# A hybrid decoder layer: another order for two mixers' products and copies, a down product with moving weights for one-tile experts, and a first projection tile by tile

## The chip, the cores and the metric

The kernel runs on one core of one Trainium2 chip. The metric is device time in microseconds (us). Engines are named as in the profile: PE is TensorE, DVE is VectorE, ACT is ScalarE, POOL is GpSimd, SP issues DMAs. All data are float32.

## What is computed

One layer for 1024 tokens of width 1024. The first part normalises the input and projects it; the columns of the projection feed two token mixers. The second part is a top-4-of-32 expert network.

```python
y = rmsnorm(h, norm_mix_g[l])
proj = y @ w_in[l]
u, v_gm, qkv, z, a, bb = jnp.split(proj, split_points, axis=-1)
out_a = gmlp_chunk_mixer(u, v_gm, gm_norm_g[l], gm_ws[l], gm_bs[l])
out_b = gated_deltanet_mixer(qkv, z, a, bb, conv_w, a_log, dt_bias, norm_g)
h = h + concatenate([out_a, out_b]) @ w_out[l]
h = h + moe_ffn(rmsnorm(h, norm_ffn_g[l]), router_w, router_b, w_gu, b_gu, w_down, b_down)
return rmsnorm(h, final_norm_g)
```

The gated DeltaNet runs over chunks of 128 tokens here. Per chunk and head it needs key-key and query-key products, the inverse of a unit lower triangular matrix (built in 7 levels, each doubling the block size), and then a step that reads the old state S, gives new values, and updates S. Each expert computes `((up + 1) * (gate * sigmoid(1.702 * gate))) @ w_down[e] + b_down[e]` for the tokens routed to it.

## The kernel before, in words

Each engine has its own instruction queue, written out by hand; semaphores tie the queues together. There are three blocks with a barrier between them.

**First block, projections.** SP loads constants, seven small parameter tensors, the eight tiles of x (128 tokens each), and then the weights of the v, u and z columns. ACT squares four tiles at a time (L312), DVE takes the mean and scales (L208, L466), POOL takes the root (L211), PE transposes (L393), and DVE copies out of PSUM into `yT` with the gain (L472). Only when all eight tiles are in `yT` does the projection begin: POOL copies each tile of `yT` into `ytile` (L270), and PE multiplies it with 512-column pieces of the weights (L408), eight products for each of v, u and z and eight narrow ones for the a and b columns. The chunk mixer's gate product (L414) closes each tile. Then come the q, k, v columns (L430) with their convolution.

**Second block, mixers.** Work goes in four pairs of chunks, i = 0 to 3, and a pair has slots s = 0 and 1 with four PSUM banks each. `start(i)` transposes the decays and betas into banks (L773, L776); `chunk(i)` makes Gk (L805) and Gq (L808), the transposed keys and values (L817, L821), the transposed lower matrix (L830), the levels (L763 and L837), and the state step: values and old state (L872, L873), state product, output (L882, L883), transposes of both mixers' outputs (L890, L894). `project` multiplies with w_out (L900). DVE turns Gk into LT (L973), Gq into AT (L975), scales keys and values (L980, L981, L983), begins the inverse (L989, L991) and updates the state (L1016). The router work of pair i-1 (`h_columns`, `logits`, `ranks`, `best_four`, `rows_of`) is spread over pair i.

**Third block, experts.** Experts are sorted by their number of tokens, and each of the 32 ranks has a fixed width: ranks 0 to 14 have two token tiles (224 down to 132 columns), ranks 15 to 31 one tile of 128. Per expert PE transposes the gathered rows (L1319), makes gate and up (L1340), and the down product (L1357). In the down product a 128 x 128 piece of the weights is stationary and the tokens' 128 columns move, so the result has features on partitions; ACT adds the bias (L1282), PE transposes back (L1328, eight of them per tile, inside the next expert's gate and up), DVE scales by the router's weight (L1477), and POOL scatters with an add (L1216). SP loads weights into six slots: each slot is loaded anew as soon as the expert before has used it (L1166 for gate and up, L1174 for down).

## Time and profile before

| quantity | value |
|---|---|
| median of 3 runs | 2508.07 us (2507.85 to 2508.09) |
| the profiled execution | 2509.08 us, of which the profile's span is 2507.2 us |
| PE busy | 2356.5 us, 94% |
| first block until the first projection product | 0 to 39.55 us |
| second block | 417.92 to 812 us |
| first transposes of the third block | 843.75 us |
| one-tile experts | about 1708 to 2472 us, 44.80 us each |

A product of float32 operands appears in the trace as two MATMUL records, a transpose as one. A row "x128" of L1357 is thus 64 products. In a timeline the distance between the starts of two rows is the time that the first took, because the end of the last instruction of a row overlaps the next. "Idle before" stands in square brackets with what ended it. PEclk is the granted TensorE clock: 1.00 is 2.4 GHz, 0.50 is 1.2 GHz.

### The profile page before, as it was taken

What the parts mean: (1) busy time and instruction counts of PE and PEld (TensorE: products, weight loads), DVE (VectorE), ACT (ScalarE), POOL (GpSimd) and SP (SyncE); (2) the same over time, 40 slices, a digit from 0 to 9 for tenths busy, and PEclk for the clock granted to TensorE, in tenths of its full rate; (3) what the DMA queues carried; (4) which work ended last, traced back from release to release, by engine and by line L of the source; (5) the groups of instructions that cost most, each with busy time, mean ns of one, the idle gap of its engine ahead of it and who ended that gap; (6) DMA issues with size and microseconds to landing.
All of it is one profiled execution on the core that took longest, in us unless ns stands there. A gap on an engine that the chain in (4) does not pass through costs nothing. (4 is left out here: it accounts for less than half of the span.)

```text
span 2507.2 us, 40183 instructions
## 1 busy us (share of the span) xinstructions
PE 2356.5 (94%) x16253; PEld 2090.4 (83%) x16254; DVE 703.4 (28%) x1627; ACT 400.7 (16%) x898; POOL 609.0 (24%) x808
## 2 busy tenths in 40 slices
PE   6999997998997599999999999999999999999994
PEld 3554444786784599999999999999999999999994
DVE  3112334445443215222222221222221212212122
ACT  2221552211211000101101111111111111111112
POOL 1112111124233312222222222232222222222222
PEclk8999999999999799999999999999999999999997
DMA  7000113010110676777788888989999999999974
GB/s 250 0 0 0 34 34 123 1 51 18 35 51 26 233 253 209 222 227 242 236 260 258 256 279 285 294 279 309 304 303 308 299 312 304 302 308 302 311 250 152
DMA packets 368902, 496.42 MB, mean 198 GB/s; under 512 B 11952, under 2 KB 281716, under 8 KB 368680
## 3 DMA queue, kind: packets, MB, share of 16 engines
q1 hardware_dynamic: 353976, 450.11, 53.9%
q0 software_dynamic: 14752, 43.84, 6.7%
q8 instruction: 127, 2.08, 0.4%
q14 instruction: 47, 0.39, 0.0%
HBM read 462.21 MB, written 34.13 MB: 198 GB/s over the span
## 5 line engine op out<-in xcount | busy, mean ns | idle before, releaser
L1340 PE MATMUL ps<-arena 128*128 128x128 f32 (+15 forms) x8192 | 1038.4, 288 | 0.8 <-DVE arena L1469 0.8
L1340 PEld LDWEIGHTS ps<-arena 128*128 128x128 f32 x8192 | 1029.6, 191 | 1.2 <-DVE arena L1469 1.0
L1357 PE MATMUL ps<-arena 128*128 128x128 f32 (+15 forms) x4096 | 521.3, 289 | 1.4 <-POOL arena L1228 1.4
L1357 PEld LDWEIGHTS ps<-arena 128*128 128x128 f32 x4096 | 515.7, 191 | 3.4 <-POOL arena L1228 1.8
L1493 DVE TENSOR_SCALAR arena<-ps,arena 128x128 f32<-128x128 f32 (+15 forms) x256 | 94.9, 371 | 1163.8 <-PE ps L1340 1160.6
L1225 POOL TENSOR_TENSOR arena<-arena 128x128 f32<-128x128 f32 (+15 forms) x256 | 133.0, 520 | 911.6 <-DVEq L1500 911.6
L1273 ACT ACTIVATE arena<-arena 128x128 f32<-128x128 f32 (+15 forms) x256 | 83.5, 326 | 1008.9 <-DVE arena L1493 1008.9
L408 PE MATMUL ps<-arena 128*128 128x512 f32 (+1 forms) x512 | 182.7, 513 | 3.9 <-POOL arena L270 3.5
L408 PEld LDWEIGHTS ps<-arena 128*128 128x128 f32 x512 | 89.0, 193 | 98.2 <-issue 94.4
L1282 ACT ACTIVATE arena<-ps,arena 128x128 f32<-128x128 f32 (+15 forms) x256 | 98.1, 383 | 448.9 <-PE ps L1357 448.9
L430 PE MATMUL ps<-arena 128*128 128x512 f32 x384 | 166.5, 592 | 0.0
L430 PEld LDWEIGHTS ps<-arena 128*128 128x128 f32 x384 | 72.8, 190 | 90.9 <-issue 90.9
L763 PE MATMUL ps<-arena 128*128 128x128 f32 x896 | 126.5, 299 | 20.4 <-DVE arena L991 14.2
L763 PEld LDWEIGHTS ps<-arena 128*128 128x128 f32 x896 | 119.8, 210 | 23.1 <-DVE arena L991 15.2
L1228 POOL TENSOR_TENSOR arena<-arena 128x128 f32<-128x128 f32 (+15 forms) x256 | 127.0, 496 | 20.1
L211 POOL TENSOR_TENSOR small<-small,cst 128x4 f32<-128x4 f32 (+1 forms) x34 | 31.0, 916 | 349.5 <-DVE small L208 349.4
L900 PE MATMUL ps<-arena 128*128 128x512 f32 x256 | 111.7, 593 | 0.0
L900 PEld LDWEIGHTS ps<-arena 128*128 128x128 f32 x256 | 47.9, 190 | 56.9 <-issue 56.9
L1494 DVE TENSOR_SCALAR arena<-ps,arena 128x128 f32<-128x128 f32 (+15 forms) x256 | 92.6, 362 | 0.0
L1203 POOL DMA_INDIRECT arena<-h_dram,arena x47 | 46.9, 998 | 176.4 <-DMA arena<-list_dram 166.0
L1216 POOL DMA_INDIRECT h_dram<-arena x47 | 74.6, 1586 | 31.9 <-issue 31.9
L1319 PE MATMUL ps<-cst,arena 128*128 128x128 f32 x376 | 48.1, 279 | 31.4 <-DMA arena<-h_dram,arena 31.3
(229 smaller groups left out, 1480.5 us busy)
## 6 DMA issues: line engine op xcount, KB each, us to landing
arena<-in_exp_w_gu SPq DMA_DIRECT2D x256, 1024.0 KB, 7.9
arena<-in_exp_w_down SPq DMA_DIRECT2D x64, 2048.0 KB, 9.1
arena<-in_x SPq DMA_DIRECT2D x16, 512.0 KB, 5.5
h_dram<-arena SPq DMA_DIRECT2D x16, 512.0 KB, 2.7
arena<-in_w_in SPq DMA_DIRECT2D x6, 1024.0 KB, 5.4
arena<-in_w_in SPq DMA_DIRECT2D x2, 2048.0 KB, 13.6
arena<-in_w_out SPq DMA_DIRECT2D x1, 4096.0 KB, 13.0
arena<-h_dram SPq DMA_DIRECT2D x8, 512.0 KB, 7.1
```

The source lines that it names most:

```text
L408: last = t_.matmul(bank(bk)[:, 0:width], ytile[s][:, k, :], wuvz[:, k, c0:c0 + width], start=(k == 0), stop=(k == KT - 1))
L430: last = t_.matmul(bank(2 * s + hf), wq[w][:, k, s * P:(s + 1) * P], yT[:, k, 512 * hf:512 * (hf + 1)], start=(k == 0), stop=(k == KT - 1))
L763: last = t_.matmul(out_bank[:, c], left[:, c], right[:, c], start=start, stop=stop)
L900: last = t_.matmul(bank(4 * s + 1 + n), mixT[s][:, k, :], wout[:, k, 512 * n:512 * (n + 1)], start=(k == 0), stop=(k == KT - 1))
L1225: v.tensor_tensor(gmn[m % 2][:, 0:n], gmn[m % 2][:, 0:n], umn[m % 2][:, 0:n], ALU.mult).then_inc(S("gum", m % 2), 1)
L1228: v.tensor_tensor(hT[:, m, 0:n], gmn[m % 2][:, 0:n], sg[m % 2][:, 0:n], ALU.mult).then_inc(S("hT"), 1)
L1273: a.activation(sg[m % 2][:, 0:n], gmn[m % 2][:, 0:n], ACT.Sigmoid, scale=ALPHA).then_inc(S("sg", m % 2), 1)
L1282: a.activation(yv[:, d, 0:n], bank(6 + d % 2)[:, 0:n], ACT.Identity, bias=bias[:, 16 + d:17 + d]).then_inc(S("yv"), 1)
L1340: last = t_.matmul(bank(m % 4)[:, q * CAP:q * CAP + n], wslot[g][:, k, 256 * q + c:256 * q + c + P], xT[:, k, 0:n], start=(k == 0), stop=( ...
L1357: last = t_.matmul(bank(6 + d % 2)[:, 0:n], wslot[g][:, k, c:c + P], hT[:, k, 0:n], start=(k == 0), stop=(k == KT - 1))
L1493: v.tensor_scalar(gmn[r][:, 0:n], bank(m % 4)[:, 0:n], of[:, m:m + 1], LIMIT, ALU.add, ALU.min).then_inc(S("gmn", r), 1)
L1494: v.tensor_scalar(umn[r][:, 0:n], bank(m % 4)[:, CAP:CAP + n], of[:, 8 + m:9 + m], LIMIT, ALU.add, ALU.min)
```

## The change

**First projection, tile by tile.** Tile 0 of x is loaded ahead of the parameters, tiles 1 and 2 between the weight loads, the rest behind them. Each tile is squared, scaled and transposed by itself; the transposes of tile t+1 stand on PE behind the v product of tile t. Products read `yT` directly, and POOL's copy into `ytile` is gone. Loops are unrolled.

**Mixers.** On PE: both Gk first, then Gq and the transposed lower matrix in turns, then the transposed values and keys. Scaled keys and values are made by ACT, per head, out of PSUM; only `ke` stays on DVE, moved to level 1. In the state step the value products of both slots come first, and the product of the queries with the old state stands between the new values' product and its use. DVE's state update no longer waits for the output product. Behind the chunk, PE runs: gates' transposes of slot 0, `start(i + 1, 1)`, values' transposes of slot 0, `start(i + 1, 0)`, the first half of slot 0's projection, both transposes of slot 1, its second half, ranks, slot 1's projection. DVE does slot 1's two copies behind `start(i + 1)`. At the end of the last pair, slot 1's residual stands ahead of `best_four(i, 0)` on DVE.

**One-tile experts.** The down product has the tokens stationary and 512 columns of the weights moving (two banks of eight products), so tokens are on partitions at once. ACT's bias step and PE's transposes back are gone. DVE adds a row of biases and then scales. SP loads that row for each of these experts, spread to 128 partitions (512 KB). Ranks 0 to 14 and the loop for overflowing experts stay as they were.

```diff
+            def load_x(t):
+                sp.dma_start(xr[:, t, :], x[0, t * P:(t + 1) * P, :]).then_inc(S("x_in", t), 16)
...
+            load_x(0)
...
+            load_x(1)
...
+            load_x(2)
...
+            for t in range(3, TT):
+                load_x(t)
...
-                    v.tensor_copy(ytile[s], yT[:, :, ds((2 * i + s) * P, P)]).then_inc(S("ytile", s), 1)
...
+            for t in range(TT):
+                if t + 1 < TT:
+                    x_root(t + 1)
+                pool.wait_ge(S("v_var"), t + 1)
...
+            def x_square(t):
+                act.wait_ge(S("x_in", t), 16)
+                if t >= 2:
+                    act.wait_ge(S("xT"), 2 * t - 2)
+                a.activation(xn[t % 2], xr[:, t, :], ACT.Square, accum_out=small[:, 20 + t % 4:21 + t % 4]).then_inc(S("x_ss"), 1)
...
+            def x_columns(t):
+                pe.wait_ge(S("xn"), t + 1)
+                for hf in range(2):
+                    q = 2 * t + hf
+                    if q >= 3:
+                        pe.wait_ge(S("xT_free"), q - 2)
+                    for k in range(4):
+                        last = t_.transpose(bank((0, 1, 7)[q % 3])[:, k * P:(k + 1) * P], xn[t % 2][:, (4 * hf + k) * P:(4 * hf + k + 1) * P], ident)
+                    last.then_inc(S("xT"), 1)
...
+                        last = t_.matmul(bank(bk)[:, 0:width], yT[:, k, t * P:(t + 1) * P], wuvz[:, k, c0:c0 + width],
+                                         start=(k == 0), stop=(k == KT - 1))
+                    last.then_inc(S(name), 1)
+                    if name == "v_proj" and t + 1 < TT:
+                        x_columns(t + 1)
...
+            def x_scale(t):
+                cell = small[:, 20 + t % 4:21 + t % 4]
+                dve.wait_ge(S("x_ss"), t + 1)
+                mean_eps(cell, D).then_inc(S("x_var"), 1)
+                dve.wait_ge(S("x_rs"), t + 1)
+                v.tensor_scalar(xn[t % 2], xr[:, t, :], cell, None, ALU.mult).then_inc(S("xn"), 1)
+
+            def x_out(t):
+                for hf in range(2):
+                    q = 2 * t + hf
+                    dve.wait_ge(S("xT"), q + 1)
+                    v.tensor_tensor(yT[:, 4 * hf:4 * hf + 4, t * P:(t + 1) * P], heads(bank((0, 1, 7)[q % 3])),
+                                    over_cols(mixg_T[:, 4 * hf:4 * hf + 4]), ALU.mult).then_inc(S("xT_free"), 1)
...
+                for s in range(2):
+                    act.wait_ge(S("vt", s), i + 1)
+                    for h in range(H):
+                        last = a.activation(vb[s][:, h * P:(h + 1) * P], bank(4 * s + 3)[:, h * P:(h + 1) * P], ACT.Copy,
+                                            scale=be_all[:, 2 * i + s, h:h + 1])
+                    last.then_inc(S("vb", s), 1)
+                for s in range(2):
+                    act.wait_ge(S("kt", s), i + 1)
+                    for h in range(H):
+                        last = a.activation(kbg[s][:, h * P:(h + 1) * P], bank(4 * s)[:, h * P:(h + 1) * P], ACT.Copy,
+                                            scale=bx_all[:, 2 * i + s, h:h + 1])
+                    last.then_inc(S("kbg", s), 1)
                 for l in range(2, LEVELS):
...
+                def lower(s):
+                    pe.wait_ge(S("LT", s), i + 1)
+                    for h in range(H):
+                        last = t_.transpose(bank(4 * s + 2)[:, h * P:(h + 1) * P], LT[s][:, h * P:(h + 1) * P], ident)
+                    last.then_inc(S("LTp", s), 1)
+
+                keys(0)
+                keys(1)
+                queries(0)
+                lower(0)
+                queries(1)
+                lower(1)
...
-                    pe.wait_ge(S("Eb", s), i + 1)
-                    for h in range(H):
-                        last = t_.transpose(bank(b0 + 3)[:, h * P:(h + 1) * P], qkvT[:, 8 + h, cols(c)], ident)
-                    last.then_inc(S("vt", s), 1)
...
+                def values(s):
+                    for h in range(H):
+                        c_ = slice(h * P, (h + 1) * P)
+                        t_.matmul(bank(4 * s)[:, c_], Um[s][:, c_], vb[s][:, c_], start=(h == 0), stop=False)
...
+                def new_state(s):
+                    pe.wait_ge(S("vn_sb", s), i + 1)
+                    four(bank(4 * s + 2), ke[s], EV[s], S("kv", s))
+                    for h in range(H):
+                        c_ = slice(h * P, (h + 1) * P)
+                        last = t_.matmul(bank(4 * s + 1)[:, c_], AT[s][:, c_], EV[s][:, c_], start=False, stop=(h == H - 1))
                     last.then_inc(S("o_ps", s), 1)
 
+                values(0)
+                values(1)
+                old_state(0)
+                new_state(0)
+                old_state(1)
+                new_state(1)
                 pe.wait_ge(S("wout_in"), 16)
-                for s in range(2):
...
+            for i in range(PAIRS):
                 chunk(i)
-                start(i + 1)
-                for n in range(2):
-                    project(i, 0, n)
+                gates_columns(i, 0)
+                if i + 1 < PAIRS:
+                    start(i + 1, 1)
+                values_columns(i, 0)
+                if i + 1 < PAIRS:
+                    start(i + 1, 0)
+                pe.wait_ge(S("mixT", 0), i + 1)
+                project(i, 0, 0)
+                gates_columns(i, 1)
+                values_columns(i, 1)
+                project(i, 0, 1)
                 if i:
                     for s in range(2):
-                        pe.wait_ge(S("EB", s), i + 2)
-                        pe.wait_ge(S("dD", s), i + 2)
+                        if i + 1 < PAIRS:
+                            pe.wait_ge(S("EB", s), i + 2)
+                            pe.wait_ge(S("dD", s), i + 2)
                         ranks(i - 1, s)
-                for n in range(2):
-                    project(i, 1, n)
+                pe.wait_ge(S("mixT", 1), i + 1)
+                if i + 1 < PAIRS:
+                    for n in range(2):
+                        project(i, 1, n)
 
...
-                    v.tensor_tensor(heads(kbg[s]), heads(bank(b0)), over_cols(bx_all[:, c, :]), ALU.mult)
-                    v.tensor_tensor(heads(ke[s]), heads(bank(b0)), heads(EV[s])[:, :, P - 1:P].broadcast_to([P, H, P]), ALU.mult)
-                    dve.wait_ge(S("vt", s), i + 1)
-                    v.tensor_tensor(heads(vb[s]), heads(bank(b0 + 3)), over_cols(be_all[:, c, :]), ALU.mult).then_inc(S("kvt", s), 1)
-                for l in range(LEVELS):
+                    v.tensor_tensor(AT[s], EV[s], bank(4 * s + 1), ALU.mult).then_inc(S("AT", s), 1)
+                    dve.drain()
+                    v.tensor_tensor(heads(Tm[s]), heads(Tm[s]), over_heads(ident), ALU.add).then_inc(S("Tl", s), 1)
+                for l in range(1, LEVELS):
+                    for s in range(2):
+                        dve.wait_ge(S("LTp", s), 7 * i + l + 1)
+                        v.tensor_tensor(heads(Pm[s]), heads(bank(4 * s + 2)), over_heads(level(l)), ALU.mult).then_inc(S("Pl", s), 1)
...
-                    dve.wait_ge(S("o_ps", s), i + 1)
...
+                states(0)
+                normed(0)
+                states(1)
+                columns(i, 0)
+                normed(1)
...
+                sp.dma_start(bd_row[r % 2], exp_b_down[0, ds(e, 1), :].rearrange("o n -> (o n)").partition_broadcast(P)
+                             ).then_inc(S("bd_in", r % 2), 16)
...
+                    for q in range(2):
+                        act.wait_ge(S("yt_ps", q), tiles_to(r + 1))
+                        act.sem_inc(S("w_used", 4 + q), 1)
+                    act.sem_inc(S("hT_free"), 1)
...
+            def down_rows(r):
+                for q in range(2):
+                    pe.wait_ge(S("w_in0", 4 + q), 16 * r + 16)
+                    pe.wait_ge(S("tr_bank", q), tiles_to(r) + 1)
+                    for k in range(KT):
+                        if q == 0:
+                            pe.wait_ge(S("hT"), 8 * r + k + 1)
+                        last = t_.matmul(bank(6 + q), hT[:, k, 0:P], wslot[4 + q][:, k, :], start=(k == 0), stop=(k == KT - 1))
+                    last.then_inc(S("yt_ps", q), 1)
...
+                if r < WIDE:
+                    down(r, WIDTHS[r], tiles_to(r), r)
+                else:
+                    down_rows(r)
...
+            def rows_out_narrow(r):
+                dve.wait_ge(S("y_out"), 16 * tiles_to(r))
+                dve.wait_ge(S("bd_in", r % 2), 16 * ((r - WIDE) // 2 + 1))
+                for q in range(2):
+                    half = yt[:, 0, 512 * q:512 * (q + 1)]
+                    dve.wait_ge(S("yt_ps", q), tiles_to(r + 1))
+                    v.tensor_tensor(half, bank(6 + q), bd_row[r % 2][:, 512 * q:512 * (q + 1)], ALU.add).then_inc(S("tr_bank", q), 1)
+                dve.drain()
+                dve.sem_inc(S("bd_used"), 1)
+                v.tensor_scalar(yt[:, 0, :], yt[:, 0, :], rec[r % 3][:, 0, 1:2], None, ALU.mult).then_inc(S("yt"), 1)
+
```

## Rows read from the trace of the kernel before

**Rows 1.** The page: PE's busy time, and granted clock in 40 slices.

```profile
PE 2356.5 (94%) x16253; PEld 2090.4 (83%) x16254; DVE 703.4 (28%) x1627; ACT 400.7 (16%) x898; POOL 609.0 (24%) x808
...
PEclk8999999999999799999999999999999999999997
```

**Rows 2.** Windows: start; mixers, plan; experts from rank 14; last: PEclk, DMA share, GB/s.

```profile
0.00:39.55 39.55, 15.12 (x75) 14.29 (x76) 20.69 (x24) 13.06 (x20) 3.29 (x8) 0.90 0.95 331
417.92:843.75 425.83, 346.31 (x2144) 278.41 (x2145) 192.91 (x408) 76.11 (x202) 139.54 (x107) 0.91 0.15 53
1663.75:2425.82 762.07, 761.81 (x6801) 760.04 (x6800) 168.37 (x514) 92.16 (x271) 184.22 (x323) 1.00 0.95 305
```

**Rows 3.** Timeline of PE, first projection: start, time, line, count.

```profile
39.55 25.32 PE L408 MATMUL ps<-arena 128*128 128x512 f32 x64 [3.54 <-POOL arena L270]
...
65.71 22.45 PE L408 MATMUL ps<-arena 128*128 128x512 f32 x64
88.01 1.14 PE L414 MATMUL ps<-arena,wsT 128*128 128x128 f32 x8
...
229.78 27.68 PE L430 MATMUL ps<-arena 128*128 128x512 f32 x64
```

**Rows 4.** Timeline of all engines, from 0 to 20 us.

```profile
7.87 0.35 PE L379 MATMUL ps<-cst,arena 68*128 68x68 f32 x1 [7.87 <-DMA arena<-in_exp_b_down]
...
11.54 0.68 DVE L456 TENSOR_TENSOR wsT<-ps,cst 128x512 f32<-128x512 f32 x1
...
17.01 1.02 POOL L211 TENSOR_TENSOR small<-small,cst 128x4 f32<-128x4 f32 x1 [16.42 <-DVE small L208]
```

**Rows 5.** Timeline of PE in the mixers: pair 0's inverse, then pair 2.

```profile
434.99 7.64 PE L763 MATMUL ps<-arena 128*128 128x128 f32 x40 [4.89 <-DVE arena L991]
...
606.64 1.05 PE L805 MATMUL ps<-arena 128*128 128x128 f32 x8
...
616.11 6.64 PE L763 MATMUL ps<-arena 128*128 128x128 f32 x32 [3.11 <-DVE arena L991]
...
656.92 1.13 PE L763 MATMUL ps<-arena 128*128 128x128 f32 x8 [0.78 <-ACT arena L733]
...
661.26 0.46 PE L872 MATMUL ps<-arena 128*128 128x128 f32 x2 [1.42 <-DVE arena L1016]
...
671.57 0.66 PE L894 MATMUL ps<-cst,arena 128*128 128x128 f32 x4 [3.29 <-POOL arena L630]
```

**Rows 6.** Timeline of DVE: the state update of pair 2, slot 0.

```profile
659.99 1.12 DVE L1016 SCALAR_TENSOR_TENSOR arena<-arena,small,ps 128x128 f32<-128x128 f32 x4 [6.84 <-PE ps L883]
```

**Rows 7.** Windows of 1 us in pair 2, columns as in Rows 2.

```profile
616.00:617.00 1.00, 0.89 (x4) 0.90 (x5) 0.93 (x3) 0.00 (x0) 0.00 (x0) 0.50 0.00 0
671.00:672.00 1.00, 0.43 (x4) 0.43 (x5) 0.96 (x2) 0.00 (x0) 0.51 (x1) 1.00 0.00 0
```

**Rows 8.** Timeline of PE in a one-tile expert.

```profile
2305.72 1.04 PE L1328 MATMUL ps<-cst,arena 128*128 128x128 f32 x8
2306.59 14.46 PE L1340 MATMUL ps<-arena 128*128 128x128 f32 x128
...
2321.76 14.63 PE L1357 MATMUL ps<-arena 128*128 128x128 f32 x128
2336.22 14.46 PE L1340 MATMUL ps<-arena 128*128 128x128 f32 x128
```

**Rows 9.** Timeline of PE, the last pair's projection of slot 0.

```profile
767.67 13.90 PE L900 MATMUL ps<-arena 128*128 128x512 f32 x32
781.41 0.30 PE L794 MATMUL ps<-arena,cst 128*128 128x32 f32 x2
```

**Rows 10.** Line L1166's eight loads in one one-tile expert, issue to landing.

```profile
DMA to landing us min/median/max: 5.4/7.8/10.5
```

**Rows 11.** Windows, with broadcast loads under way; columns as in Rows 2.

```profile
33.00:36.00 3.00, 3.00 (x19) 2.77 (x17) 2.18 (x3) 0.00 (x0) 0.00 (x0) 0.68 1.05 395
```

**Rows 12.** Timeline of all engines, the last expert's down product and scatter.

```profile
2455.28 1.73 PE L1357 MATMUL ps<-arena 128*128 128x128 f32 x14
...
2458.14 12.99 PE L1357 MATMUL ps<-arena 128*128 128x128 f32 x114 [1.13 <-POOL arena L1228]
...
2474.80 1.58 POOL L1216 DMA_INDIRECT h_dram<-arena  x1 [16.72 <-issue]
```

387 lines of the change are left out of this document (168 added, 219 removed).

## The prediction

> **What bounds the kernel.** I read the page first. PE is busy for 94% of the span at the full clock nearly throughout [rows 1], so a gain must come from PE: less work, or fewer waits. The windows by stage then say where which of the two lies [rows 2]. In the one-tile experts (and the one before them) PE is busy for 761.81 of 762.07 us: no wait is left, only work can go. The mixers with the plan have 346 of 426 us busy and a mean clock of 0.91: waits and a slow clock. The first 39.55 us hold 15 us of PE work. I then read PE's timeline in each of the three, for what stands at its head and what ends each wait.
>
> **First projection.** PE begins its products at 39.55 us and leaves them at 229.78 [rows 3]. What must come first in the new order is tile 0 only. The parameters now stand behind one tile of x: 0.52 MB at 331 GB/s [rows 2] is 1.6 us, so PE's parameter transposes go from 7.87 to 9.5 us and DVE's last parameter copy, which ended 4.35 us behind their start, from 12.2 to 13.8 us [rows 4]. Behind it come mean and root (0.3 + 1.02 us), scaling (about 0.7), four transposes, and two copies of 0.68 us, in all 5 us: products could begin at 18.8 us. The v weights have 4.3 MB up to and with them, 13 us at 331 GB/s plus about 4 us of start and landing: 17 us, so not the last to come, but near it. I take 18.8, bounds 18 to 24. The u weights end at 6.9 MB and the z weights at 9.6 MB, 23 to 31 us at that rate, and are needed at about 28 and 36.
>
> The loop gets longer: seven of the eight tiles now carry eight transposes on PE, 0.87 us (the count and time of L1328 [rows 8]). The first tile costs 26.16 us at the slow clock, plus 0.87: 45.8. Six tiles cost 23.28 (65.71 to 88.01, and 0.98 for the gate product) plus 0.87, the last 23.28: 168.2. So the loop ends at 214.0 instead of 229.78: **15.8 us less**. The new wait on PE is for the scaled tile t+1 behind the v product of t. Its square stands on ACT behind the z step of tile t-1, and its scaling on DVE behind that tile's gate product. From the end of the z product I add up about 6.7 us until the tile is ready, while PE has 1.8 us of narrow products, 0.9 of gate product and 6.9 us of v product (16 records of 0.434) to do, 9.6 us. It is hidden; if the margin of 3 us went, each tile would pay the excess. POOL's copy was off the path but at the head. Bounds for this part: 10 to 18.
>
> **Mixers, the inverse's beginning.** Pairs 1 to 3 repeat one pattern. From the first Gk product PE takes 9.8 us of work to the end of level 1, waits 3.11 us for DVE, and then runs 32 records in 6.5 us that take 3.57 at full clock, since the clock has fallen to 0.50 [rows 5, 7]. DVE was late because six scalings (0.68 us each) stood before the inverse. In the new order DVE has per slot three operations between the transposed lower matrix and the first T; slot 0's is ready about 5.5 us behind the chunk's start, when PE is still at its transposed keys (till 6.3), slot 1's at 7.5, when PE comes at 7.2. That leaves 0.4 us of wait, too short to bring the clock down as 3.11 us did. ACT's sixteen small copies begin as the values' transposes come (5.2 us); the first is needed at 8.4 and the keys' at 9.3 on DVE, so this is hidden with 1 to 2 us, about one copy's worth of error. DVE's queue then holds `ke` between two levels, but PE has the eight router transposes there. Gain: 3.1 + 2.9 - 0.5 = 5.5 us in each of three pairs. Pair 0 had a wait of 4.89 us and 40 slow records; its chain begins at the same LT and saves three operations and the queue before them, 5.3 us. Sum 21.8.
>
> **Mixers, the state step.** Per pair PE waited 0.78 for the copied new values (twice), 1.42 for the state, 3.29 for the mixed output of slot 1 [rows 5]: 6.3 us. In place of them: the copy (0.6 us and its latencies) is covered by eight records of the query product, 0.89 us: 0.1 each. The state update takes 1.12 us [rows 6] and now starts behind the state product, with eight records in between: a wait of 0.65. Slot 0's mixed output takes 5.0 us from its last output product by DVE, POOL, DVE, POOL; PE has in that time the whole state step of slot 1 and one `start`, 5.7 us: hidden. Slot 1's has all of half a projection, 6.9 us. What is late next is DVE: with slot 1's copies put behind `start(i + 1)`, its `best_four` of both slots end about 0.8 us behind the point where PE comes to `ranks`. Left: 1.75 us, or 0.95 in pair 0. Gains 5.3 + 4.5 + 4.5. The last pair has no `start` to cover the copy into `mixT`, which then costs about 1 us, and in its tail `best_four(i, 0)` goes behind a residual, another 0.5: 5.1. Sum 19.4. Nothing is added to PE. Mixers together: **41.2 us less**, bounds 28 (the slow clock stays, or my small waits are each double) and 46.
>
> **One-tile experts.** The old down product took 14.46 us for 128 records, and the transposes back 0.87 [rows 8]. The new one is 32 records with 512 moving columns; the output projection has just that form and took 13.74 us [rows 9]. So 0.72 + 0.87 = 1.59 us per expert, 16 times: 25.4. The last expert has more: its wait of 1.13 us goes, as the eighth product now comes 6 us behind the first instead of 1.6, and the way from the last product to the scatter (bias, wait, transposes, scaling, 3.8 us [rows 12]) loses its detour for an addition and one more scaling, about 0.9. So 0.7 + 1.1 + 0.9 plus the transposes' issue: 3.2. **28.6 us less.** DVE has 2.2 instead of 1.4 us at one place of each expert, inside a 3.6 us step in which it has 1 us to do. ACT has less.
>
> The load of the bias row is the cost here. An expert's traffic is 305 GB/s times 44.80 us, 13.7 MB, with a DMA share of 0.95 [rows 2]; it becomes 14.2 MB in 43.2 us, 328 GB/s. Where broadcasts of this kind were under way, 395 GB/s were moved at a share of 1.05 [rows 11], so the row costs about 1.3 us of DMA time and the share would come to 1.01, under what it has reached. And a slot's load lands at most 10.5 us behind its issue [rows 10], while it is used some 37 us behind it: about 27 us of lead, which even a deficit of 1 us per expert would not eat up in 17 experts. I take no cost, with an upper bound of 20 us.
>
> **Sum.** 15.8 + 41.2 + 28.6 = 85.6. The profiled execution took 2509.08 us (span 2507.2 and 1.9 around it), which gives 2423.5; its distance to the median of the runs, 1.0, gives **2423 us**. What a measurement here can tell from no change is 0.2%, 5 us.
>
> **Rivals.** (A) The clock in the mixers stays slow. In the new order the transposes of the lower matrix, values and keys stand in nearly one row, 2.2 us, and behind the state step 2.6 us of them. Against it: at 671 us PE had done nothing but transposes and waiting for 5 us, and had the full clock [rows 7]. For it: at 616 it had not, with 2.7 us of transposes ahead of the wait. If each pair pays 2.9 us once, 11.6 us: 2435. Chance 0.15. The Trainium skill ("TensorE: Matmul & The Clock Gate", Part 4: PE-mode transpose) says that transposes do not count as activity for the clock in the way that other products do, which speaks for this rival; the row at 671 us does not agree with it, the one at 616 us would.
> (B) The DMA becomes the bound of the one-tile experts, because scatters and gathers move worse than the mean share tells. It would give back 10 to 25 us: about 2440. Chance 0.08.
> (C) The projection starts late for want of weights or stalls at the scaled tiles, 5 to 8 us: 2430. Chance 0.12.
> (D) The other side: slower. One mechanism: the bias row, one 4 KB row read 128 times, moves so badly that loads run out of their lead. The experts would have to give back 85.6 us and use up 27 us of lead, in 17 experts 6.6 us each over the new 43.2, so 49.8 us of DMA time per expert. The loads now take about 0.95/1.05 of 44.8, 40.5 us; the row would need over 9 us, under 60 GB/s, where rows 11 show 395. Chance 0.02.
> (E) A stall that I do not see in the reordered queues, or no net change: 0.01 for no change within 0.2%, and a further 0.02 of it for losses over 30 us.
>
> **Numbers.** My forecast, within 2413 to 2433, has 0.60. The range 2411 to 2444 takes in A, C and most of B. Every case but D and E is faster by more than 0.2%: faster 0.96, same 0.01, slower 0.03.
>
> **What would show it.** Right: the first L408 product (under its new line) at 18 to 20 us; loop over at about 214; no wait over 1 us at the first levels of pairs 1 to 3 and their records at 0.11 us each; pair period of 93 to 96 us down by 10; one-tile experts 43.2 us apart with PE busy throughout, 32 records in 13.7 us and a DMA share near 1.0. Wrong: PE waiting for DMA or in the v product's shadow, PEclk 0.50 behind a chunk's transposes, a wait for `ranks` or `mixT` over 1 us, or one-tile experts at more than 43.5 us.

## The result, and the profile after

The kernel after takes **2423.8 us** in the median (2422.1 to 2426.41, 4 runs), the kernel before 2507.96 in the same comparison; the ratio is **0.9662, 95% interval 0.9649 to 0.9675**. The forecast was 2423. The profiled execution took 2422.1 us (span 2420.3).

The spans differ by 86.9 us. PE's timeline says in which stage, by the starts of the first q/k/v product, of the first mixer transpose and of the first transpose of the experts:

| stage | before | after | difference | predicted |
|---|---|---|---|---|
| start to the first q/k/v product | 229.78 | 213.06 | -16.7 | -15.8 |
| q/k/v products, barrier | 188.14 | 187.65 | -0.5 | 0 |
| mixers and plan | 425.83 | 386.78 | -39.05 | -41.2 |
| experts to the end | 1663.45 | 1632.81 | -30.6 | -28.6 |

The page's busy line and granted clock, against [rows 1]. PE is busy for 41 us less (less work, and less of it at the slow clock) and its span is 87 us shorter, so about half of the gain was waiting:

```profile
PE 2315.3 (96%) x14485; PEld 1923.4 (79%) x14486; DVE 709.1 (29%) x1642; ACT 365.5 (15%) x825; POOL 602.5 (25%) x806
...
PEclk9999998999996999999999999999999999999997
```

The windows of the mixers with the plan, and of nearly sixteen periods of the one-tile experts, against [rows 2]. The second is busy for all of its 686.25 us, at a DMA share of 1.01:

```profile
400.71:787.49 386.78, 339.07 (x2145) 272.72 (x2145) 187.87 (x392) 92.83 (x266) 140.09 (x107) 0.92 0.16 58
1663.75:2350.00 686.25, 686.25 (x4695) 563.80 (x4694) 164.72 (x491) 39.26 (x126) 169.82 (x301) 1.00 1.01 328
```

PE's timeline of the first projection, against [rows 3]. The products begin at 18.60; the next tile's transposes (L389, 0.88 us) stand behind the v product without a wait; the first tile lasts to 44.85, the later ones 24.15 us each:

```profile
18.60 9.12 PE L401 MATMUL ps<-arena 128*128 128x512 f32 x16 [0.83 <-issue]
27.56 1.04 PE L389 MATMUL ps<-cst,arena 128*128 128x128 f32 x8
28.44 15.58 PE L401 MATMUL ps<-arena 128*128 128x512 f32 x48
43.88 1.14 PE L409 MATMUL ps<-arena,wsT 128*128 128x128 f32 x8
44.85 7.03 PE L401 MATMUL ps<-arena 128*128 128x512 f32 x16
...
213.06 27.20 PE L425 MATMUL ps<-arena 128*128 128x512 f32 x63
```

PE's timeline of pair 2, against [rows 5]: the start of the chunk, slot 1's first level, the router's products (L795) and what follows them, slot 1's product with the state, the ranks:

```profile
570.96 2.10 PE L811 MATMUL ps<-arena 128*128 128x128 f32 x16
...
577.30 1.15 PE L769 MATMUL ps<-arena 128*128 128x128 f32 x8
579.26 2.94 PE L769 MATMUL ps<-arena 128*128 128x128 f32 x22 [0.82 <-DVE arena L1022]
...
602.22 3.66 PE L795 MATMUL ps<-rw,arena 128*128 128x32 f32 x32
605.71 1.48 PE L769 MATMUL ps<-arena 128*128 128x128 f32 x8
...
619.87 1.13 PE L895 MATMUL ps<-arena 128*128 128x128 f32 x8 [0.41 <-DVE arena L1048]
...
640.99 0.30 PE L800 MATMUL ps<-arena,cst 128*128 128x32 f32 x2
641.13 0.39 PE L801 MATMUL ps<-arena,cst 128*128 128x32 f32 x2
```

The wait of 3.11 us has become 0.82, and the 24 records from there to the router's first transposes take 3.0 us, at a granted clock of 1.00 from 579 to 582 us, where the 32 behind the old wait took 6.5 us. But the 8 records behind the router's products have 1.28 us to the start of the next row, where 8 have 0.9 at full clock: there the clock still falls, as it did in pair 2 of before. The state's waits (0.78, 1.42, 3.29) have left one of 0.41, and the view shows none ahead of the ranks.

The timeline of one-tile experts, against [rows 8]: a period of 43.20 us, and the transposes of L1374 are those of the gathered rows. Behind them the last expert's scatter, against [rows 12]: 16.29 us behind the start of its down product (2372.81), where it was 19.52:

```profile
2200.91 13.90 PE L1407 MATMUL ps<-arena 128*128 128x512 f32 x32
2214.64 28.75 PE L1395 MATMUL ps<-arena 128*128 128x128 f32 x256
2243.23 1.04 PE L1374 MATMUL ps<-cst,arena 128*128 128x128 f32 x8
2244.10 13.90 PE L1407 MATMUL ps<-arena 128*128 128x512 f32 x32
...
2389.10 1.58 POOL L1265 DMA_INDIRECT h_dram<-arena  x1 [13.85 <-issue]
```

### The profile page after: what moved, and what is told of

The parts are those of the page before. It is cut to its first block, busy times and chain, and to the rows that moved or that the text cites. A ratio compares the mean times of both kernels' runs of the same rounds, so it can differ in the third digit from the quotient of the medians.

```text
span 2420.3 us, 36350 instructions
## 1 busy us (share of the span) xinstructions
PE 2315.3 (96%) x14485; PEld 1923.4 (79%) x14486; DVE 709.1 (29%) x1642; ACT 365.5 (15%) x825; POOL 602.5 (25%) x806
## 4 chain that ended last, share of the span: by engine, by line
PE 64%; issue 2%; DMA 1%; POOL 1%; DVE 0%; POOLq 0%; DVEq 0%; ACT 0%; SPq 0%; ACTq 0%
PE ps L1395 41%; PE ps L1422 11%; PE ps L1407 9%; PE ps L1374 2%; PE ps L1383 1%; DMA arena<-h_dram 0%; DMA h_dram<-arena 0%; DMA arena<-list_dram 0%; DMA arena<-h_dram,arena 0%; POOL small L210 0%; POOL arena L1274 0%; DVE arena L1625 0%; POOL arena L1277 0%; POOL h_dram L1265 0%; DVE arena L1537 0%
## 5 line engine op out<-in xcount | busy, mean ns | idle before, releaser
L1395 PEld LDWEIGHTS ps<-arena 128*128 128x128 f32 x8192 | 1029.6, 191 | 8.8 <-issue 7.7
L1395 PE MATMUL ps<-arena 128*128 128x128 f32 (+15 forms) x8192 | 1035.7, 288 | 0.8 <-DVE arena L1537 0.8
L1422 PE MATMUL ps<-arena 128*128 128x224 f32 (+14 forms) x1920 | 272.5, 303 | 0.1
L1422 PEld LDWEIGHTS ps<-arena 128*128 128x128 f32 x1920 | 270.1, 189 | 0.3 <-POOL arena L1277 0.3
L1407 PE MATMUL ps<-arena 128*128 128x512 f32 x544 | 236.3, 592 | 0.0
L1407 PEld LDWEIGHTS ps<-arena 128*128 128x128 f32 x544 | 102.0, 190 | 122.0 <-issue 122.0
L425 PE MATMUL ps<-arena 128*128 128x512 f32 x384 | 166.5, 592 | 0.0
L401 PEld LDWEIGHTS ps<-arena 128*128 128x128 f32 x512 | 88.1, 192 | 90.9 <-issue 90.9
L425 PEld LDWEIGHTS ps<-arena 128*128 128x128 f32 x384 | 72.8, 190 | 90.9 <-issue 90.9
L769 PE MATMUL ps<-arena 128*128 128x128 f32 x896 | 118.3, 284 | 2.5 <-DVE arena L1022 2.5
L769 PEld LDWEIGHTS ps<-arena 128*128 128x128 f32 x896 | 110.3, 195 | 4.4 <-DVE arena L1022 3.2
L937 PE MATMUL ps<-arena 128*128 128x512 f32 x256 | 112.7, 595 | 0.8 <-DVE arena L1069 0.8
L210 POOL TENSOR_TENSOR small<-small,cst 128x1 f32<-128x1 f32 (+1 forms) x40 | 33.4, 838 | 321.1 <-DVE small L207 321.0
L937 PEld LDWEIGHTS ps<-arena 128*128 128x128 f32 x256 | 47.6, 190 | 56.5 <-issue 55.0
L1331 ACT ACTIVATE arena<-ps,arena 128x224 f32<-128x224 f32 (+14 forms) x120 | 48.1, 401 | 242.5 <-PE ps L1422 242.5
```

The costliest lines, as they stand in the source:

```text
L401: last = t_.matmul(bank(bk)[:, 0:width], yT[:, k, t * P:(t + 1) * P], wuvz[:, k, c0:c0 + width], start=(k == 0), stop=(k == KT - 1))
L425: last = t_.matmul(bank(2 * s + hf), wq[w][:, k, s * P:(s + 1) * P], yT[:, k, 512 * hf:512 * (hf + 1)], start=(k == 0), stop=(k == KT - 1))
L769: last = t_.matmul(out_bank[:, c], left[:, c], right[:, c], start=start, stop=stop)
L937: last = t_.matmul(bank(4 * s + 1 + n), mixT[s][:, k, :], wout[:, k, 512 * n:512 * (n + 1)], start=(k == 0), stop=(k == KT - 1))
L1395: last = t_.matmul(bank(m % 4)[:, q * CAP:q * CAP + n], wslot[g][:, k, 256 * q + c:256 * q + c + P], xT[:, k, 0:n], start=(k == 0), stop=( ...
L1407: last = t_.matmul(bank(6 + q), hT[:, k, 0:P], wslot[4 + q][:, k, :], start=(k == 0), stop=(k == KT - 1))
```

## The experiments

The kernel after was run again with some of them (2422.64 us, 2420.6 to 2425.03; ratio 0.9649, 0.9636 to 0.9662), and this value is the one that variants of it are compared with.

> The changed kernel once more, for the comparisons of this group: ratio 0.966.

### Each part alone

Three kernels take one block's functions from the kernel after and the others from before:

```diff
 # proj_alone: first block, before -> after
-                    v.tensor_copy(ytile[s], yT[:, :, ds((2 * i + s) * P, P)]).then_inc(S("ytile", s), 1)
+                    if name == "v_proj" and t + 1 < TT:
+                        x_columns(t + 1)
 # mixers_alone: second block, before -> after
+                keys(0)
+                keys(1)
+                queries(0)
+                lower(0)
 # experts_alone: third block, before -> after
-                down(r, WIDTHS[r], tiles_to(r), r)
+                    down_rows(r)
```

> The kernel before with the new first block alone. Sum of the parts: the first q, k, v product begins 16.7 us earlier (213.1 us, as in the changed kernel, against 229.8), so 16 to 17.5 us less than before, ratio about 0.9935. Rival (the parts depend on each other, or it was the mixers that gained from data laid elsewhere): less than 12 or more than 20.

> The kernel before with the new mixer block alone. Sum of the parts: 39 us less (the changed kernel's stretch from its first mixer product to its first expert product is 386.8 us against 425.8), ratio about 0.9845. The phase at which the clock falls in the router products may move it by 2 to 4 us. Rival: the waits come back when the block starts at another time, 30 us or less.

> The kernel before with the new down product for one-tile experts alone. Sum of the parts: 28.6 us by my count, 30.6 by the difference of the two traces behind the first transposes of the experts; ratio 0.988. One-tile experts 43.2 us apart. Rival: 25 or less, with the rest of the 30.6 from elsewhere.

| kernel | median us | ratio, interval | less than before | that stage in its own trace |
|---|---|---|---|---|
| projection alone | 2496.95 | 0.9948, 0.9931 to 0.9964 | 12.5 | -16.45 |
| mixers alone | 2469.66 | 0.9836, 0.9819 to 0.9852 | 39.8 | -38.65 |
| experts alone | 2479.16 | 0.9884, 0.9867 to 0.9901 | 30.3 | -30.2 |

The three sum to 82.6 us against 84 to 89 for the whole, and their stages to 85.3 us against 86.4 in the trace of the whole: within the intervals, the parts add up. The mixers and the experts came out as expected. The projection alone, in the median, misses the 16 to 17.5 us that were expected of it, though its own stage gives 16.45. In its trace the rest went in code that it does not touch: its mixers took 429.29 us against 425.83, and its experts 2.6 us more. Of the mixers' 3.5 us, 2.9 are lost in pair 1. Its timeline there shows where: behind a wait that the kernel before has too, transposes that take 0.44 us from start to start take 0.85, and 32 records that take 13.90 us [rows 9] take 14.77:

```profile
560.10 1.12 PE L885 MATMUL ps<-cst,arena 128*128 128x128 f32 x4 [3.29 <-POOL arena L621]
561.01 1.06 PE L764 MATMUL ps<-cst,gc_all 128*128 128x128 f32 x4
...
564.42 14.77 PE L891 MATMUL ps<-arena 128*128 128x512 f32 x32
```

So TensorE's clock fell at another place than in the kernel before. That is taken up with the pairs below. Why the experts took longer is not known; the eight traces with the same new expert code have 1632.6 to 1635.3 us for that stage, so a difference of 3 us there between two traces shows nothing.

### Is the bias row free, and how far does it stay so?

Two kernels load the row again, into buffers that nobody reads, three and six times per one-tile expert (the six in two groups, one of them among the gate and up weights):

```diff
                 sp.dma_start(bd_row[r % 2], exp_b_down[0, ds(e, 1), :].rearrange("o n -> (o n)").partition_broadcast(P)
                              ).then_inc(S("bd_in", r % 2), 16)
+                for d in range(3):
+                    if r > WIDE:
+                        sp.wait_ge(S("spare_in", d), 16 * (r - WIDE))
+                    sp.dma_start(spare[d], exp_b_down[0, ds(e, 1), :].rearrange("o n -> (o n)").partition_broadcast(P)
+                                 ).then_inc(S("spare_in", d), 16)
```

> The changed kernel with three more loads of the bias row per one-tile expert, into buffers that nobody reads: 1.6 MB more, about 4.0 us of DMA time at 395 GB/s. Theory (DMA demand of 40.5 to 41.5 us per expert now fits under 43.2, and a lead of 27 us is there to be used up): demand 44.5 to 45.5, a deficit of 1.3 to 2.3 us, 22 to 39 us over 17 experts less the lead: PE begins to wait only in the last few experts, 0 to 12 us slower than the changed kernel. Rival (no lead: a late load delays at once): 22 to 39 us slower, waits in every expert. Rival (DMA far from its bound): no change.

> The kernel after, with six more loads of 512 KB per one-tile expert (the bias row again, into three buffers that nobody reads, each filled twice: once among the gate and up weights and once behind the own bias row); nothing else is changed. With three more such loads the transfers ran at 356 GB/s and 1.07 of the engines' span, and the products never waited. Theory (the transfers' limit is near 356 GB/s; until it is passed, and beyond it until the lead of the prefetched slots is used up, more bytes cost nothing): 328 GB/s over 43.2 us are 14.2 MB per expert, with 3.15 MB more 17.3 MB, which takes 48.6 us at 356 GB/s; 5.4 us short per expert, 92 us over 17 experts, less the lead of some 27 us: 50 to 75 us slower than the kernel after (ratio to the kernel before about 0.985 to 0.995), the first experts still at 43.2 us and the later ones near 48.6 us. Rival (the transfers can go at 395 GB/s, the rate that one window of the kernel before showed): 43.8 us per expert, within the lead, so under 5 us slower, and a rate near 395 GB/s in the stage.

Three more: **2424.5 us** (2421.28 to 2426.03), the same as the kernel after. The theory (0 to 12 us slower) and the rival of transfers far from their bound (no change) both allow that; the kernel with six more tells them apart. Six more: **2479.77 us** (2477.22 to 2480.64), 57 us slower, inside the 50 to 75 of the theory and far outside the rival's 5. The window of the stage with three more, and two with six more, with the rate as the last number:

```profile
1700.00:2350.00 650.00, 650.00 (x4462) 535.21 (x4461) 155.42 (x465) 37.41 (x120) 158.88 (x283) 1.00 1.07 357
```

```profile
1700.00:1894.00 194.00, 193.49 (x1366) 162.34 (x1364) 48.43 (x145) 11.84 (x38) 48.40 (x88) 1.00 1.06 361
1964.00:2400.00 436.00, 401.39 (x2669) 324.17 (x2670) 93.31 (x279) 22.42 (x72) 94.54 (x169) 0.99 1.06 360
```

Both run at 357 to 361 GB/s, and this is the limit in this stage. With three more rows PE was busy for all of 650 us although the loads were already at it: the queues fell behind by some 0.9 us per expert (15.7 MB asked for, 15.4 moved), which the lead absorbed. With six more, the timeline of PE shows four periods of 43.2 us, then the first late load, and from there on about three waits for a load in each expert:

```profile
1894.54 5.62 PE L1408 MATMUL ps<-arena 128*128 128x128 f32 x48 [0.90 <-DMA arena<-in_exp_w_gu]
...
2253.82 2.02 PE L1408 MATMUL ps<-arena 128*128 128x128 f32 x16 [1.60 <-DMA arena<-in_exp_w_gu]
2257.97 21.70 PE L1408 MATMUL ps<-arena 128*128 128x128 f32 x192 [2.13 <-DMA arena<-in_exp_w_gu]
```

The last ten periods are 48.07 us in the mean, against 48.6 worked out from bytes and rate. Each is 4.9 us over 43.2, and the first late load came 4.9 experts behind the first one-tile expert's down product (1683.09): the lead was about 24 us by this estimate (4.9 times 4.9), and I had read some 27 from [rows 10]. The Trainium skill ("DMA: Bandwidth & Descriptors", Specifications) gives about 358 GB/s as a core's limit from HBM; by that rule, the trace agrees, with 360. The 395 GB/s that a 3 us window of the kernel before showed [rows 11] was not reached in the experts. It is no limit for every kind of traffic: from 403 to 420 us of the kernel after, where w_out and x are loaded while small buffers in DRAM are filled, 438 GB/s were moved. What sets the two stretches apart was not tested.

### The inverse's beginning: what made slot 1's wait 0.82 us

The prediction had 0.4. DVE's and POOL's timelines of the kernel after in pair 2:

```profile
575.03 0.68 DVE L1020 TENSOR_TENSOR arena<-arena,ps 128x512 f32<-128x512 f32 x1
575.80 1.43 DVE L1022 TENSOR_TENSOR arena<-arena,cst 128x512 f32<-128x512 f32 x1
...
578.52 0.69 DVE L1022 TENSOR_TENSOR arena<-arena,cst 128x512 f32<-128x512 f32 x1
```

```profile
575.41 1.28 POOL L611 TENSOR_TENSOR arena<-arena,cst 128x512 f32<-128x512 f32 x1
576.76 1.60 POOL L613 TENSOR_TENSOR arena<-cst,arena 128x512 f32<-128x512 f32 x1
```

The addition of the identity (L1022, both inputs from SBUF) takes 1.43 us for slot 0 and 0.69 for slot 1. The first one starts inside a POOL operation that ends at 576.69, and itself ends at 577.23, near the 577.4 that 0.69 us behind that end would give. In front of it stands the masking AT (L1020), whose result nothing needs before the output products; only the router's first transposes, behind level 1, wait for the bank that it reads. The kernel `at_behind` puts AT behind both first T; `tail_order` puts the last pair's `best_four(i, 0)` ahead of slot 1's residual again; `at_tail` has both:

```diff
-                    dve.wait_ge(S("Gq", s), i + 1)
-                    v.tensor_tensor(AT[s], EV[s], bank(4 * s + 1), ALU.mult).then_inc(S("AT", s), 1)
                     dve.drain()
                     v.tensor_tensor(heads(Tm[s]), heads(Tm[s]), over_heads(ident), ALU.add).then_inc(S("Tl", s), 1)
+                for s in range(2):
+                    dve.wait_ge(S("Gq", s), i + 1)
+                    v.tensor_tensor(AT[s], EV[s], bank(4 * s + 1), ALU.mult).then_inc(S("AT", s), 1)
...
             h_mean(i, 0)
-            residual(i, 1)
             best_four(i, 0)
+            residual(i, 1)
```

> The changed kernel with the last pair's best_four(i, 0) ahead of slot 1's residual on DVE, as it was before. In the changed kernel PE waits 3.57 us for that mask (744.39 us) and comes to slot 1's transposes 4.4 us behind the end of the projection; the kernel before needed 3.2 us. Theory: the moved residual costs 1.3 us, so this is 1 to 2 us faster than the changed kernel. Rival (the mask was late for POOL's share of the port, not for the order; POOL's two passes would now lie across best_four again): no change or slower by up to 1 us.

> As tail_order, and AT (query product times decay) on DVE behind both slots' first T instead of between. Theory: the 0.82 us wait for slot 1's T (579.26 us, in pairs 1 to 3) is two copies of 0.6 us late and goes: 2 to 3 us less than tail_order. Rival: the next wait takes its place, since the ACT copies of the keys or the products TP are as late: 0 to 0.5 us.

> The kernel after, with the masking of the query products (AT) moved on VectorE behind both slots' first T; nothing else is changed. Theory (slot 1's T waits for an operation that nothing needs until the output products; this and not the order of the tail is what made the version with both edits 4 us faster): 0.4 us less wait in each pair, and where the clock then stays up behind it some 1.6 us more: 3 to 5 us faster than the kernel after, level with the version with both edits (ratio to before near 0.963). Rival (the two edits are each worth half): 1 to 2 us faster.

Tail order: **2423.79 us** (2421.3 to 2425.26), no change. Both: **2418.56** (2417.76 to 2420.28). AT alone: **2417.65** (2417.41 to 2419.97; ratio 0.9632, 0.9618 to 0.9646), about 5 us faster than the kernel after and level with both; no run of it is as slow as the fastest of the kernel after. The rival of two halves is out. Against the trace of the kernel after, the beginnings of pairs 1 to 3 are each 0.8 us shorter and pair 0 is 0.3 us shorter, 2.6 us in all; another 1.6 us are the end of pair 2's inverse, which ran at full clock here. The wait for slot 1's T is gone, and one of 0.37 for the next step's masked product (L1027), which now stands behind both AT, has come in its place. PE's timeline of that kernel in pair 2, first level and behind the router's products:

```profile
578.00 2.02 PE L769 MATMUL ps<-arena 128*128 128x128 f32 x16 [0.37 <-DVE arena L1027]
...
599.82 3.66 PE L795 MATMUL ps<-rw,arena 128*128 128x32 f32 x32
603.31 1.14 PE L769 MATMUL ps<-arena 128*128 128x128 f32 x8
```

The same 32 router records (3.66 us) come first in both kernels, but the eight records behind them have 0.97 us to the next row's start here and 1.28 in the kernel after. Windows of the kernel after, during the router's last products and behind them, give its clock, 1.00 and then 0.60:

```profile
603.00:605.70 2.70, 2.70 (x26) 2.70 (x26) 0.11 (x1) 0.00 (x0) 0.00 (x0) 1.00 0.00 0
605.70:610.00 4.30, 4.30 (x26) 4.30 (x26) 0.90 (x2) 0.60 (x1) 0.00 (x0) 0.60 0.00 0
```

Why the tail's order gained nothing: DVE's and POOL's timelines of `tail_order` have `best_four(i, 0)` begun at 738.67, 2.8 us earlier than in the kernel after (741.46), but across POOL's two passes of the router norm:

```profile
740.44 2.29 DVE L1088 CAST arena<-small 128x4 f32<-128x4 uint32 x1
742.80 0.29 DVE L1090 TENSOR_TENSOR arena<-cst,arena 128x128 f32<-128x128 f32 x1
...
743.45 1.28 DVE L1076 TENSOR_TENSOR arena<-arena,ps 128x512 f32<-128x512 f32 x2
```

```profile
740.36 2.34 POOL L633 TENSOR_TENSOR arena<-arena,ffn_g 128x1024 f32<-128x1024 f32 x1
```

A cast of four columns, 0.17 us elsewhere, lasts 2.29 us, to the end of POOL's operation. The Trainium skill ("SBUF — State Buffer", Who interferes with whom) says that a cast can contend with GpSimd for a pair of ports that the first to come holds for its whole instruction, and that a DVE operation with both inputs in SBUF contends with GpSimd's reads; by that rule, the trace agrees, in the cast here (end 742.73, POOL's 742.70) and in the addition of 1.43 us above.

### The copies on ACT, and the early state update

`copies_dve` gives the scaled keys and values back to DVE, behind the first T, and keeps PE's new order. `state_late` gives DVE's state update its wait back:

```diff
 # copies_dve
-                        last = a.activation(vb[s][:, h * P:(h + 1) * P], bank(4 * s + 3)[:, h * P:(h + 1) * P], ACT.Copy,
+                    v.tensor_tensor(heads(vb[s]), heads(bank(4 * s + 3)), over_cols(be_all[:, 2 * i + s, :]), ALU.mult).then_inc(S("vb", s), 1)
 # state_late
                     dve.wait_ge(S("egl", s), i + 1)
+                    dve.wait_ge(S("o_ps", s), i + 1)
```

> The changed kernel with the scaled keys and values made by DVE again, behind the first T, ACT's sixteen small copies left out. Theory (moving them to ACT is worth what DVE is late at level 1): by the queues T at level 1 comes about 2.4 us later and PE waits 1.5 to 2 us per pair: 5 to 9 us slower than the changed kernel. Rival (only their place ahead of T mattered, not the engine): no more than 1 us slower. If the wait reaches 3 us the clock falls too and it is 15 or more.

> The kernel after, with VectorE's state update waiting for the slot's output products again, as in the kernel before; nothing else is changed. Theory (the early state update is worth 0.9 us in each pair, as the step of the state showed in my working: slot 1's product with the state waits for slot 0's update, which then starts only behind eight more products): 3 to 4 us slower than the kernel after, 0.7 to 1.0 us per pair, and the wait ahead of slot 1's products back at 1.4 us or more. Rival (slot 1's other operand, the negated W from ScalarE, comes as late): no difference above 1 us.

Copies on DVE: **2428.18 us** (2425.8 to 2432.07; ratio 0.9673), 5.5 us slower, within the 5 to 9 that were expected. The wait was not: 1.5 to 2 us per pair were expected, and pairs 1 and 2 have 0.7 more of it and are each 0.4 to 0.5 us shorter than in the kernel after, since the end of their inverse ran at full clock. In the trace, 2.1 us of the loss lie in pair 0 and 3.2 in pair 3, so the time is right in part by luck. PE's timeline of pair 2 has a second wait where the kernel after has none:

```profile
581.76 1.16 PE L757 MATMUL ps<-arena 128*128 128x128 f32 x8 [0.82 <-DVE arena L1010]
583.65 2.02 PE L757 MATMUL ps<-arena 128*128 128x128 f32 x16 [0.73 <-DVE arena L1017]
```

State update late: **2429.17 us** (2427.65 to 2430.36; ratio 0.9675), 6.5 us slower, where 3 to 4 were expected. The rival (nothing above 1 us) is out. The wait is back at 1.41, exactly 1.0 us more:

```profile
621.24 1.13 PE L895 MATMUL ps<-arena 128*128 128x128 f32 x8 [1.41 <-DVE arena L1049]
```

The step from the new values to the projection is 1.0 us longer in pairs 0 to 2 (13.40 against 12.40) and 1.7 in the last (13.37 against 11.68), 4.7 us in all, so the mechanism is right and its size was put a little low. Of the 7.2 us between the two profiled spans, 3.3 lie in the last pair (1.6 of them at the end of its inverse, where the clock was 0.86) and 2.5 in the experts, which is within what that stage differs by between traces of equal code; why the inverse's end was slow here stays open.

### Does the idle stretch bring the clock down?

`filler` is the kernel before with twelve more products per pair, put where PE waits 3.1 us for slot 0's T. Nobody reads them:

```diff
+                            if l == 1 and s == 0:
+                                pe.wait_ge(S("AT", 0), i + 1)
+                                for _ in range(3):
+                                    for h in range(H):
+                                        t_.matmul(bank(1)[:, h * P:(h + 1) * P], qkvT[:, 4 + h, cols(2 * i)],
+                                                  qkvT[:, h, cols(2 * i)], start=True, stop=True)
                             pe.wait_ge(S("Tl", s), 6 * i + l)
```

> The kernel before, with twelve more products of 128 columns per pair (24 records, about 2.7 us, into a bank whose contents have been read; nobody reads them) where the products of the inverse's first level wait 3.1 us for slot 0's T; nothing is taken away. Theory (it is that idle stretch that brings TensorE's clock down behind it, 6.64 us for 32 records instead of 3.7): with the stretch filled the clock stays at 1.00 there, and the kernel is faster than before by 2.9 us in each of three to four pairs, 8 to 12 us, although it computes more. Rival (the clock falls for what came earlier, the sixteen transposes or the router's products, or the wait's length is only its sign): the slow records stay, and the time is that of the kernel before or up to 2 us more.

**2504.72 us** (2501.13 to 2508.03, 12 runs; ratio 0.9979, 0.9969 to 0.9989): more work, and 4 us less time. PE's timeline of pair 2, the filling products (L837) and the first level:

```profile
616.27 2.84 PE L837 MATMUL ps<-arena 128*128 128x128 f32 x24
619.55 1.16 PE L763 MATMUL ps<-arena 128*128 128x128 f32 x8 [0.44 <-DVE arena L997]
620.91 1.27 PE L763 MATMUL ps<-arena 128*128 128x128 f32 x9 [0.21 <-DVE arena L997]
```

The window of the first records has a granted clock of 1.00, where it was 0.50 [rows 7]:

```profile
619.00:622.00 3.00, 2.35 (x18) 2.06 (x18) 2.38 (x4) 0.00 (x0) 0.00 (x0) 1.00 0.01 3
```

So filling those 3 us kept the clock up behind them, as the theory has it; the rival is out. But the 8 to 12 us that the theory gave did not come. The beginning of pairs 1 to 3 became only 1.1, 2.1 and 2.1 us shorter and not 2.9: in pair 1 the slow clock had cost less (32 records in 5.65 us), and at full clock PE waits for DVE inside the level (0.21 above). The next table shows the rest.

### The pairs side by side

From PE's timelines, us: from the chunk's first product to the router's first transposes (the inverse's beginning), from the router's products to the values (the end of the inverse), from the values to the projection (the state step), and the whole pair.

| kernel, pair | beginning | end of inverse | state step | pair |
|---|---|---|---|---|
| before, 1 | 14.96 | 10.02 | 19.75 | 93.04 |
| before, 2 | 15.95 | 11.65 | 19.74 | 95.66 |
| filler, 1 | 13.83 | 11.66 | 21.71 | 96.26 |
| filler, 2 | 13.83 | 11.65 | 19.73 | 93.54 |
| projection alone, 1 | 15.03 | 10.01 | 21.70 | 95.93 |
| after, 1 and 2 | 11.30 | 11.65 | 12.40 | 84.74 |
| at_behind, 1 | 10.53 | 11.65 | 12.39 | 83.94 |
| at_behind, 2 | 10.52 | 10.01 | 12.39 | 82.30 |
| copies_dve, 2 | 12.05 | 10.02 | 12.39 | 84.22 |
| state_late, 1 | 11.31 | 10.01 | 13.40 | 84.11 |
| state_late, 2 | 11.31 | 11.66 | 13.39 | 85.73 |

The end of the inverse has the same products in all of them, and takes either 10.0 or 11.65 us; in the kernel before the granted clock was 1.00 there in pair 1 (549 to 559 us) and 0.85 in pair 2. Which of the two it is differs between pairs of one kernel that run the same instructions. The state step of the old order likewise is 19.74 or 21.7. These are places where the clock may fall, and when one fall is prevented another may come, later in the pair: in pair 1 `filler` saved 1.1 us at the beginning and lost 1.6 and 2.0 behind it. A pair is thus worth its sum to plus or minus some 2 us. What decides where a fall comes, with the same instructions and the same waits, no run here shows.

## Why the prediction was right

The likeliest case came in, and its three sums are each within 2.2 us of the trace. That the whole is within 1 us is in part luck: against the trace the forecast has 0.9 and 2.0 us too little in the first projection and the experts, 2.2 too much in the mixers, and nothing for the 0.5 of the q, k, v products. Its last step comes to 2422.5 and was written as 2423.

**First projection.** Right in each step. Products begin at 18.60 (18.8 predicted), the extra transposes cost 0.87 us per tile (24.15 against 23.28), and no v product is followed by a wait. The 0.9 us over the prediction is the first tile, 26.25 us instead of 27.03, and the 0.2 at its start. Rival C is out.

**The inverse's beginning.** The mechanism was right: the long wait goes, and the clock stays up behind the short one. Two terms of it were mis-sized. "That leaves 0.4 us of wait" became 0.82, because I took 0.7 us for each DVE operation and one of them waited out a POOL operation; with AT moved, this wait is gone, and one of 0.37 for the next operation is left. And the 2.9 us for the slow clock were read from pair 2: in pair 1 the same 32 records took 5.65 us, 1.9 over, and at the end of the inverse pair 1 of the kernel after lost 1.6 us (11.65 against 10.02). So pair 1 gave 8.3 us and pair 2 10.9, where 10.0 stood for each. The row of pair 1 in the kernel before:

```profile
523.07 5.65 PE L763 MATMUL ps<-arena 128*128 128x128 f32 x32 [3.11 <-DVE arena L991]
```

Pair 0 gave 10.5 (10.6 predicted), though it has a wait of 3.62 us in it for its first LT.

**The state step.** Per pair 6.3 us of waits left 0.41; I had left 1.75 in pairs 1 and 2. The 0.8 for the ranks was too dear (no wait), as were the 0.1 for each copy, and the state's 0.65. The state step gained 7.35 us and the stretch behind it, which took over half of the transposes, grew by 1.07: 6.3 net against the predicted 4.5. This over-run of 1.8 us is as large as what the beginning fell short of in pair 1 (1.85; in pair 2 0.85), so the pair's sum looks better than its terms. The early state update is worth 1.0 us of it in pairs 0 to 2, which `state_late` shows. The last pair gave 9.7 (10.6 predicted), and its terms are off by more: up to its projection it gained 12.4 us, 1.6 of them at the end of the inverse by the clock, and behind that it lost 2.8. Of these, 1.0 are the transposes that moved there and 1.6 a longer wait for slot 0's mask (3.57 us at 744.39, where it was 1.98). The prediction blamed the order of the tail with 0.5; `tail_order` shortens that wait to 2.55 us, and its time does not change.

**Rival A** (the clock stays slow in the mixers) holds in a part that I had not priced: not behind the chunk's transposes, where the clock is full in every pair from 1 on, but behind the router's products and, in pair 0, behind the wait of 3.62 us (0.66 from 411 to 416 us). The rule that I had set beside it from the Trainium skill ("TensorE: Matmul & The Clock Gate", Part 4: PE-mode transpose) does not show here: 2.2 us of them at a chunk's start and 2.7 us behind the state step are followed by records at full clock (0.11 us each of 128 columns, 0.43 of 512).

**One-tile experts.** 43.20 us each, as worked out, and 3.23 us at the last expert against 3.2. The 2 us over the prediction are mostly at the ends of the stage: 0.3 before the first gate product, 1.2 behind the last scatter, and 0.5 between the first gate product and the last down product. That the bias row is free is shown by three more of it at no cost, and by the six that are not: the loads now have room for about 1.3 MB per expert (29 to 32 GB/s over 43.2 us) before they run at their limit, and a lead of 24 us behind that. Rivals B and D are out.

**What stays open.** Inside the mixers only AT, the copies on ACT, the early state update and the tail's order were tested by themselves. What the order of the key, query and lower-matrix products and that of `start` are each worth is argued from the waits that left. The parts of the first projection (the order of the loads, the copy that is gone) were not run apart either.

The version that the experiments point to, AT behind both first T, is the fastest that was run: 2417.65 us, ratio 0.9632 to the kernel before.

## What to carry to other kernels

A wait of a few microseconds on PE can cost twice, once for itself and once for the clock behind it: 3.11 us did so in all three passes of the kernel before, and 3.29 us behind the state step did so in three passes of the projection alone and in none of the kernel before. Price both, and then check that the fall is gone and not moved: compare the same stretch in several repetitions of the loop before a gain of 2 us is booked to an edit. In a hand-ordered queue, look for the operation that stands in front of what PE waits for and is needed much later. And a stage with prefetched slots can run at its transfer limit for a long while without a sign on PE, so ask for the rate of the window, not only for the waits.

## What was not expected of the hardware

- Twelve products that nobody reads made the kernel 4 us faster, since TensorE kept 1.00 of its clock instead of 0.50 behind them.
- The same instructions took 10.0 or 11.65 us in neighbouring pairs of one execution, at a granted clock of 1.00 or 0.85.
- A DVE cast of 128 x 4 elements took 2.29 us beside a POOL operation on SBUF, against 0.17 without it, and an addition of 128 x 512 elements 1.43 against 0.69.
- The bias row, 4 KB read 128 times, was no dearer for the DMA engines than other loads: with three and six more of it the rate was 357 and 360 GB/s at a DMA share of 1.06 to 1.07, and without them 328 at 1.01.
